# Expert matmuls in pairs of units: the fp32r products of both units first, then the bf16 products of both

## The chip, the cores and the metric

The kernel runs on one core of one Trainium2 chip. The metric is the device time of one execution in microseconds; before the change the median of three runs is 2556.29 us (2554.6 to 2564.03). A core has several engines, each with its own instruction queue that runs in order: TensorE (PE in the profile, with its weight loads as PEld) multiplies matrices into PSUM, ScalarE (ACT) and VectorE (DVE) work on tiles, GpSimd (POOL) issues the gathers and scatters here, SyncE (SP) issues the loads of weights. They synchronise by semaphores: an instruction raises a counter when it is done, and another queue waits for a value of it.

## The reference

One encoder layer for two request groups of 16 + 512 tokens with shared weights (float32, width 1024): a combined projection, differential attention, a bidirectional mLSTM, an output projection, and then the part that this change touches, a mixture of experts in which each expert chooses its tokens:

```python
aff = softmax(xt @ w_router)              # 16 experts
gate, idx = lax.top_k(aff.T, cap)         # cap = 66 tokens of each group
def expert(args):
    ids, wg, wu, wd = args                # (1024, 2816), (1024, 2816), (2816, 1024)
    xg = xt[ids]
    return (jax.nn.silu(xg @ wg) * (xg @ wu)) @ wd
y = zeros.at[idx].add(expert outputs * gate)
```

Each expert thus multiplies 132 rows (66 of each group) by two matrices of 1024 x 2816 and one of 2816 x 1024.

## The kernel before, in words

The change lies in `experts` (from L1591), the last stage. The kernel keeps float32 accuracy by splitting both operands. A weight w is split into a high half in the format fp32r (`whi`) and a rest in bf16 (`wlo`); the rows are split into a high and a low half in fp32r that stand side by side in `xx` (264 columns), with a bf16 copy of the rows in `xb` (132 columns). One product of weights is then two matmuls into the same PSUM bank: `whi` times the 264 columns in fp32r, and `wlo` times the 132 columns in bf16, added onto the first 132.

An expert is cut into 34 units (`UNITS`). Units 0 to 21 are "up" units: unit u = 2t + kind computes 256 columns of the gate matrix (kind 0) or of the up matrix (kind 1), as 2 x 8 matmuls of each format into two PSUM banks. An expert's up units use four of the eight banks (`bank_set`), so that unit u + 2 goes into the banks of unit u. Units 22 to 33 are "down" units, with 16 or 12 matmuls of each format; six of them add into one set of four banks (`dg` 0), six into the other (`dg` 1). What an up unit leaves is summed in two steps: ScalarE copies the right half of the two banks to `low` (`copy_low`, L1832), and VectorE adds the left half to it into `gs` or `us` (`add_low`, L1945), which raises `sum_ready`. Then ScalarE's silu (L1839) and VectorE's product (`gate`, L1951) make the hidden rows, which both engines split (L1844, L1845, L1957) for the down units.

The weights come in pieces of up to 2 MB through a ring of five `raw` buffers, issued by SyncE as soon as VectorE has done the last split of the piece that the buffer held. For each unit n ScalarE makes `whi` (`split_high`, L1822), and VectorE `wlo` from it (`split_low`, L1916). Both halves have rings of five (`R_SPLIT`), so split_high(n) waits until unit n - 5 is done.

The order of each queue is written out by hand. TensorE runs its units in order; an up unit waits for `sum_ready` of unit u - 2 (L1742), then for `whi`, and before its bf16 matmuls for `wlo` (L1752). After units 2 to 5 it transposes a part of the previous expert's outputs (`turn_outputs`, L1795), after unit 23 the next expert's rows (`turn_rows`, L1732). ScalarE and VectorE have a loop over the same steps u. In step u ScalarE does: copy_low(u - 1); split_high of the units up to `made(ex, u)` (L1650), which is u plus a lead of 4, 3 or 2 units (`lead`, L1646: 4 for u < 6 and u >= 30, 3 for 6 to 12 and 27 to 29, 2 for 13 to 26), so one unit in most steps, none in steps 6 and 13, two in steps 27 and 30; then silu in odd steps or the split of the hidden rows in even ones; then, in steps 3 to 6, `gated_rows` (L1877). VectorE does in step u: add_low(u - 1); `gate` in even steps; the split of the hidden rows in odd ones; and then split_low of the same unit as ScalarE's split_high of that step.

The code below has the line numbers of the profile.

Of the kernel before, what the change touches and what calls it, by code (L numbers as in the profile page):

```python
# [57 lines left out]
N_EXP = 16  # L58
# [87 lines left out]
def build(nc, x_meta, x_prompt, x_sample, g_mix, w_in, b_gates, conv_w, g_q, g_k, lams, g_da, g_ml,  # L146
          w_out, g_ffn, w_router, w_gate, w_up, w_down, rope_cos, rope_sin, out, xn_rows, zv_rows, stages=5):
    with ExitStack() as ctx:
# [70 lines left out]
        if stages >= 5:  # L219
            experts(nc, locals())  # L220
# [1044 lines left out]
UNITS_UP = 22  # L1265
DOWN_PARTS = ((0, 4), (4, 4), (8, 4), (12, 4), (16, 3), (19, 3))
UNITS = UNITS_UP + 2 * len(DOWN_PARTS)
# [323 lines left out]
def experts(nc, e):  # L1591
# [17 lines left out]
    low = [tiles(f"low{i}", [P, 2, C2]) for i in range(2)]  # L1609
# [30 lines left out]
    TURN_X = UNITS_UP + 1  # L1640
    SPLIT_X = TURN_X + 2
    DG0_END, DG1_END = UNITS_UP + 6, UNITS
    OUT_STEPS = {2: 0, 3: 1, 4: 2, 5: 3}
    FETCH, ADD = 13, 7

    def lead(u):  # L1646
# [7 lines left out]
    def bank_set(ex):  # L1654

        return 4 * (ex % 2)

    def other_set(ex):

        return 4 - bank_set(ex)  # L1660

    def shaped(t, u):

        cols = 256 if u < UNITS_UP else 512
        n = KD if u < UNITS_UP else DOWN_PARTS[(u - UNITS_UP) % 6][1]
        return t[:, 0:n * cols].rearrange("p (k f) -> p k f", f=cols)
# [5 lines left out]
    with nc.Block() as block:  # L1672

        @block.sync
        def _(sp):
            for q in range(NR, PIECES * N_EXP):
                ex, p = divmod(q - NR, PIECES)
                sp.wait_ge(lo_ready, UNITS * ex + LAST_UNIT[p] + 1)
                load_piece(sp, e, raw, loaded, q)
            sp.wait_ge(added, 32 * N_EXP)  # L1680
# [31 lines left out]
        @block.tensor  # L1712
        def _(pe):
            for c in range(NC5):
                at = PT + CCOL[c]
                mm = pe.transpose(banks(0, G * N_EXP)[:, at:at + CROWS[c]], AFF[0:CROWS[c], c], ident[0:CROWS[c], 0:CROWS[c]])  # L1716
            mm.then_inc(aT_done, 1)
            pe.wait_ge(ranked, 1)
            for i, t in enumerate((vals, indexf)):
                mm = pe.transpose(banks(2, CAP)[:, 32 * i:32 * i + 32], t[:, 0:CAP], ident[0:G * N_EXP, 0:G * N_EXP])  # L1720
            mm.then_inc(lists_done, 1)

            def turn_rows(ex):

                pe.wait_ge(xg_loaded, 32 * ex + 32)
                if ex >= 1:
                    pe.wait_ge(sum_ready, UNITS_UP * ex)
                b = other_set(ex)
                for k in range(KD):
                    for g in range(G):  # L1730
                        at = 512 * (k // 3) + (k % 3) * C2 + CAP * g
                        mm = pe.transpose(banks(b)[:, at:at + CAP], xg[:, g, k * P:(k + 1) * P], ident[0:CAP, 0:CAP])  # L1732
                mm.then_inc(xT_done, 1)

            def up(ex, u):

                t, kind = divmod(u, 2)
                n = UNITS * ex + u
                if t == 0 and kind == 0:
                    pe.wait_ge(xl_ready, ex + 1)  # L1740
                if t >= 1:
                    pe.wait_ge(sum_ready, UNITS_UP * ex + 2 * (t - 1) + kind + 1)  # L1742
                elif ex >= 1:
                    pe.wait_ge(yT_ready, 2 * ex - 1)
                pe.wait_ge(hi_ready, n + 1)
                b = bank_set(ex) + 2 * kind
                w = shaped(whi[n % R_SPLIT], u)
                for i in range(2):
                    for k in range(KD):
                        pe.matmul(banks(b + i)[:, 0:2 * C2], w[:, k, i * P:(i + 1) * P], xx[:, k], start=(k == 0), stop=False,  # L1750
                                  skip_group_check=True)
                pe.wait_ge(lo_ready, n + 1)  # L1752
                w = shaped(wlo[n % R_SPLIT], u)
                for i in range(2):
                    for k in range(KD):
                        mm = pe.matmul(banks(b + i)[:, 0:C2], w[:, k, i * P:(i + 1) * P], xb[:, k], start=False, stop=(k == KD - 1),  # L1756
                                       skip_group_check=True)
                mm.then_inc(unit_done, 1)

            def down(ex, u):  # L1760

                dg, d = divmod(u - UNITS_UP, len(DOWN_PARTS))
                c0, cn = DOWN_PARTS[d]
                n = UNITS * ex + u
                b = (other_set(ex), bank_set(ex))[dg]
                if d == 0 and dg == 0 and ex >= 1:
                    pe.wait_ge(yr_ready, 4 * ex)
                if d == 0 and dg == 1:
                    pe.wait_ge(sum_ready, UNITS_UP * (ex + 1))
                    if ex + 1 < N_EXP:  # L1770
                        pe.wait_ge(xl_ready, ex + 2)
                if dg == 0:
                    pe.wait_ge(hl_ready, PAIRS * ex + (c0 + cn + 1) // 2)
                pe.wait_ge(hi_ready, n + 1)
                w = shaped(whi[n % R_SPLIT], u)
                for c in range(cn):
                    for i in range(HD2):
                        pe.matmul(banks(b + i)[:, 0:2 * C2], w[:, c, i * P:(i + 1) * P], hx[:, c0 + c], start=(c0 + c == 0), stop=False,  # L1778
                                  skip_group_check=True)
                pe.wait_ge(lo_ready, n + 1)  # L1780
                w = shaped(wlo[n % R_SPLIT], u)
                for c in range(cn):
                    for i in range(HD2):
                        mm = pe.matmul(banks(b + i)[:, 0:C2], w[:, c, i * P:(i + 1) * P], hb[:, c0 + c], start=False,  # L1784
                                       stop=(c0 + c == M - 1), skip_group_check=True)
                mm.then_inc(unit_done, 1)

            def turn_outputs(ex, i):

                g, half = divmod(i, 2)  # L1790
                if i == 0:
                    pe.wait_ge(yT_ready, 2 * ex + 2)
                b = bank_set(ex) + i
                for k in range(HD2):
                    mm = pe.transpose(banks(b, CAP)[:, k * P:(k + 1) * P], yT[:, HD2 * half + k, CAP * g:CAP * (g + 1)], ident[:])  # L1795
                mm.then_inc(y_done, 1)

            turn_rows(0)
            for ex in range(N_EXP):
                for u in range(UNITS):  # L1800
                    if u < UNITS_UP:
                        up(ex, u)
                    else:
                        down(ex, u)
                    if u in OUT_STEPS and ex >= 1:
                        turn_outputs(ex - 1, OUT_STEPS[u])
                    if u == TURN_X and ex + 1 < N_EXP:
                        turn_rows(ex + 1)
            for i in range(4):
                turn_outputs(N_EXP - 1, i)  # L1810

        @block.scalar
        def _(act):
# [33 lines left out]
            def split_rows(ex):  # L1847

                act.wait_ge(xT_done, ex + 1)
                if ex >= 1:  # L1850
                    act.wait_ge(unit_done, UNITS * (ex - 1) + UNITS_UP)
                b = other_set(ex)
                two = banks(b)[:, 0:1024].rearrange("p (b n) -> p b n", b=2)[:, :, 0:3 * C2].rearrange("p b (k n) -> p b k n", k=3)
                one = banks(b + 2)[:, 0:2 * C2].rearrange("p (k n) -> p k n", k=2)
                for t in (xx, xb):
                    nc.scalar.activation(t[:, 0:6, 0:C2].rearrange("p (b k) n -> p b k n", b=2), two, ACT.Copy)
                    last = nc.scalar.activation(t[:, 6:8, 0:C2], one, ACT.Copy)
                last.then_inc(xh_ready, 1)
# [9 lines left out]
            def gated_rows(ex, i):  # L1868

                g, half = divmod(i, 2)  # L1870
                act.wait_ge(y_done, 4 * ex + i + 1)
                if i == 0:
                    if ex + 1 < N_EXP:
                        act.wait_ge(xT_done, ex + 2)
                    else:
                        act.wait_ge(added, 32 * ex)
                nc.scalar.activation(yr[:, g, 512 * half:512 * (half + 1)], banks(bank_set(ex) + i, CAP)[:, 0:512], ACT.Copy,  # L1877
                                     scale=gateT[:, g, ex:ex + 1]).then_inc(yr_ready, 1)
# [6 lines left out]
            for ex in range(N_EXP):  # L1885
                for u in range(UNITS):
# [13 lines left out]
                    if u == SPLIT_X and ex + 1 < N_EXP:  # L1900
                        split_rows(ex + 1)
                    if u - 1 in OUT_STEPS and ex >= 1:
                        gated_rows(ex - 1, OUT_STEPS[u - 1])
            copy_ylow(N_EXP - 1, 1)
# [126 lines left out]
```

## Time and profile before

| | us |
|---|---|
| median of three runs | 2556.29 |
| the profiled execution | 2560.51 |
| its span, first to last instruction | 2558.7 |
| TensorE matmuls, busy | 2412.1 (94%) |
| VectorE, busy | 1934.0 (76%) |
| ScalarE, busy | 1697.3 (66%) |
| split_low (`wlo`, L1916), 436 + 108 instructions | 963.6 + 240.5 |
| split_high (`whi`, L1822), 436 + 108 instructions | 804.9 + 201.5 |

Times in the profile are microseconds from the span's start. A row of the timeline gives the start, the length, the engine, the line of the code, the operation, what it writes and reads with shapes, how many instructions are merged (x16), and in brackets how long the engine was idle before it and what released it. A row of the busy times gives the stretch, its length, then for PE, PEld, DVE, ACT and POOL the busy time with the number of instructions, then the clock that TensorE was granted (1.00 is 2.4 GHz, 0.50 is 1.2 GHz), the busy share of the DMA engines and GB/s. A row of the waits gives who waited for whom: the total, how often, and the longest. The ends of matmuls are modelled, so starts, above all those of weight loads, are the better marks.

### The profile page before, as it was taken

Reading aid. Unit: us, or ns where it says so; the run is one execution under the profiler, and the core shown is the slowest. Engines: PE = TensorE matmul, PEld = TensorE weight load, DVE = VectorE, ACT = ScalarE, POOL = GpSimd, SP = SyncE. Lnnn points to the kernel's source line nnn. Section 1 sums busy time; section 2 is a strip of 40 time slices with the busy share of each in tenths; the row PEclk is TensorE's granted clock in tenths of the full one; section 3 lists DMA queues with packets and bytes.
Section 4 is the critical chain, followed back from the end, with each engine's and each line's share of the span. In section 5 each row is a group of like instructions: output and inputs, shape, how many; then the busy total and the mean of one; then the engine's idle time right before and its main releaser. Section 6 shows DMA issues by size and latency. Waiting matters only on the chain.

```text
span 2558.7 us, 51699 instructions
## 1 busy us (share of the span) xinstructions
PE 2412.1 (94%) x21830; PEld 2206.4 (86%) x21830; DVE 1934.0 (76%) x2311; ACT 1697.3 (66%) x2379; POOL 265.6 (10%) x174
## 2 busy tenths in 40 slices
PE   7999997998979929999999999999999999999997
PEld 5777884785757729999999999999999999999997
DVE  4621035884873359999998998998999999989986
ACT  7311224573443228888888888887888888888885
POOL 3312111110122010000000000000000000000000
PEclk9999996896889959999999999999999999999999
DMA  4122101001023359999999999999999999999993
GB/s 124 33 86 81 66 17 35 1 13 56 1 91 123 116 187 321 366 362 349 366 360 350 381 346 352 379 344 366 366 349 365 362 348 368 360 348 383 345 365 127
DMA packets 325114, 624.33 MB, mean 244 GB/s; under 512 B 11828, under 2 KB 48788, under 8 KB 324884
## 3 DMA queue, kind: packets, MB, share of 16 engines
q1 hardware_dynamic: 317220, 602.78, 66.2%
q0 software_dynamic: 7664, 18.25, 3.6%
q8 instruction: 173, 2.83, 0.5%
q14 instruction: 57, 0.47, 0.1%
HBM read 597.23 MB, written 23.69 MB: 243 GB/s over the span
## 4 chain that ended last, share of the span: by engine, by line
PE 59%; issue 3%; DVE 1%; DMA 1%; POOL 0%; ACT 0%; POOLq 0%
PE ps L1750 26%; PE ps L1778 13%; PE ps L1756 13%; PE ps L1784 6%; PE ps L1795 1%; PE ps L1732 1%; POOL xg L1693 0%; DMA xg<-xn_rows,idxT 0%; DVE vals L1924 0%; DVE index L1927 0%; DMA out_rows<-yr,idxT 0%; DVE aff L1926 0%; POOL out_rows L1701 0%; POOLq L1672 0%; PE ps L1716 0%
## 5 line engine op out<-in xcount | busy, mean ns | idle before, releaser
L1916 DVE TENSOR_TENSOR wlo<-raw,whi 128x2048 bf16<-128x2048 f32 (+1 forms) x436 | 963.6, 2223 | 55.0 <-ACT whi L1822 55.0
L1822 ACT ACTIVATE whi<-raw 128x2048 fp32r<-128x2048 f32 (+1 forms) x436 | 804.9, 1859 | 37.6 <-PE ps L1784 37.6
L1750 PE MATMUL ps<-xx,whi 128*128 128x264 f32 x4512 | 616.2, 289 | 3.6 <-DVE xx L1967 3.6
L1750 PEld LDWEIGHTS ps<-xx,whi 128*128 128x128 f32 x4512 | 564.2, 189 | 3.8 <-DVE xx L1967 3.8
L1756 PE MATMUL ps<-xb,wlo 128*128 128x132 bf16 x4512 | 313.7, 221 | 0.0
L1778 PE MATMUL ps<-hx,whi 128*128 128x264 f32 x2256 | 312.3, 290 | 0.0
L1778 PEld LDWEIGHTS ps<-hx,whi 128*128 128x128 f32 x2256 | 283.8, 189 | 0.0
L1756 PEld LDWEIGHTS ps<-xb,wlo 128*128 128x128 bf16 x4512 | 264.0, 97 | 13.8
L1916 DVE TENSOR_TENSOR wlo_last<-raw,whi_last 128x2048 bf16<-128x2048 f32 (+1 forms) x108 | 240.5, 2227 | 13.6 <-ACT whi_last L1822 13.6
L1832 ACT ACTIVATE low<-ps 128x264 f32<-128x264 f32 x352 | 137.7, 391 | 135.7 <-PE ps L1756 122.0
L1822 ACT ACTIVATE whi_last<-raw 128x2048 fp32r<-128x2048 f32 (+1 forms) x108 | 201.5, 1866 | 9.3 <-PE ps L1784 9.3
L1701 POOL DMA_INDIRECT out_rows<-yr,idxT x32 | 48.4, 1512 | 1235.8 <-ACT yr L1877 1231.0
L1784 PE MATMUL ps<-hb,wlo 128*128 128x132 bf16 x2256 | 157.0, 221 | 0.0
L1750 PE MATMUL ps<-xx,whi_last 128*128 128x264 f32 x1120 | 154.1, 290 | 0.0
L444 PE MATMUL ps<-w_hi,h_hi 128*128 128x512 f32 (+1 forms) x360 | 144.3, 401 | 4.5 <-POOL w_lo L314 4.5
L444 PE MATMUL ps<-w_hi,h_lo 128*128 128x512 f32 (+1 forms) x360 | 141.6, 393 | 0.0
L444 PE MATMUL ps<-w_lo,h_hi 128*128 128x512 f32 (+1 forms) x360 | 141.6, 393 | 0.0
L1750 PEld LDWEIGHTS ps<-xx,whi_last 128*128 128x128 f32 x1120 | 141.2, 189 | 0.0
L1784 PEld LDWEIGHTS ps<-hb,wlo 128*128 128x128 bf16 x2256 | 130.1, 98 | 7.7
L1945 DVE TENSOR_TENSOR gs<-ps,low 128x264 f32<-128x264 f32 x176 | 74.9, 426 | 30.7 <-ACT low L1832 30.7
L522 ACT ACTIVATE w_hi<-w 128x1024 fp32r<-128x1024 f32 x28 | 29.4, 1054 | 103.5 <-DMA w<-in_w_in 103.5
L671 DVE TENSOR_SCALAR cy<-zp,cols 128x1056 f32<-128x1056 f32 x8 | 6.2, 770 | 120.8 <-ACT zp L581 120.8
(236 smaller groups left out, 3463.4 us busy)
## 6 DMA issues: line engine op xcount, KB each, us to landing
raw<-in_w_gate SPq DMA_DIRECT2D x80, 2048.0 KB, 12.7
raw<-in_w_up SPq DMA_DIRECT2D x80, 2048.0 KB, 10.3
raw<-in_w_down SPq DMA_DIRECT2D x64, 2048.0 KB, 10.7
raw<-in_w_down SPq DMA_DIRECT2D x32, 1536.0 KB, 8.1
raw<-in_w_gate SPq DMA_DIRECT2D x16, 1024.0 KB, 9.0
raw<-in_w_up SPq DMA_DIRECT2D x16, 1024.0 KB, 11.6
w<-in_w_in SPq DMA_DIRECT2D x28, 512.0 KB, 4.9
zv_rows<-qn SPq DMA_DIRECT2D x24, 256.0 KB, 2.0
```

The source lines that it names most:

```text
L444: mm = pe.matmul(banks(4 + i % 3, ZROWS[c])[:, 0:512], h, w, start=(k == 0 and i3 == 0), stop=(k == KD - 1 and i3 == 2))
L522: nc.scalar.activation(w_hi[u % NW][:], w_whole[u % NW][:], ACT.Copy).then_inc(w_high, 1)
L1701: nc.gpsimd.indirect_dma_start(out, bass.IndirectOffsetOnAxis(ap=idxT[:, g, ex:ex + 1], axis=0), yr[:, g, :], None, compute_op=ALU.add).th ...
L1732: mm = pe.transpose(banks(b)[:, at:at + CAP], xg[:, g, k * P:(k + 1) * P], ident[0:CAP, 0:CAP])
L1750: pe.matmul(banks(b + i)[:, 0:2 * C2], w[:, k, i * P:(i + 1) * P], xx[:, k], start=(k == 0), stop=False, skip_group_check=True)
L1756: mm = pe.matmul(banks(b + i)[:, 0:C2], w[:, k, i * P:(i + 1) * P], xb[:, k], start=False, stop=(k == KD - 1), skip_group_check=True)
L1778: pe.matmul(banks(b + i)[:, 0:2 * C2], w[:, c, i * P:(i + 1) * P], hx[:, c0 + c], start=(c0 + c == 0), stop=False, skip_group_check=True)
L1784: mm = pe.matmul(banks(b + i)[:, 0:C2], w[:, c, i * P:(i + 1) * P], hb[:, c0 + c], start=False, stop=(c0 + c == M - 1), skip_group_check=True)
L1822: nc.scalar.activation(shaped(whi[n % R_SPLIT], u), unit_raw(raw, ex, u), ACT.Copy).then_inc(hi_ready, 1)
L1832: nc.scalar.activation(low[u % 2][:], src, ACT.Copy).then_inc(low_ready, 1)
L1916: nc.vector.tensor_tensor(shaped(wlo[n % R_SPLIT], u), unit_raw(raw, ex, u), shaped(whi[n % R_SPLIT], u).bitcast(F32), ALU.subtract).then_ ...
L1945: nc.vector.tensor_tensor((gs, us)[kind][:], src, low[kind][:], ALU.add).then_inc(sum_ready, 1)
```

## The change

On TensorE's queue `up` is cut into `up_high` (the fp32r matmuls, with the waits for the banks and for `whi`) and `up_low` (the wait for `wlo` and the bf16 matmuls, which raise `unit_done`); `down` likewise. The loop goes over pairs of units. The steps after which the outputs are transposed become the odd units 3, 5, 7 and 9; `OUT_STEPS` is also read by ScalarE, whose `gated_rows` move from steps 3 to 6 to steps 4, 6, 8 and 10. `TURN_X` is 23, so the next expert's rows are transposed at the same place as before. Nothing else of ScalarE's and VectorE's order changes, and each matmul is the same as before.

```diff
-    OUT_STEPS = {2: 0, 3: 1, 4: 2, 5: 3}
+    OUT_STEPS = {3: 0, 5: 1, 7: 2, 9: 3}
...
-            def up(ex, u):
+            def up_high(ex, u):
...
+            def up_low(ex, u):
+
+                n = UNITS * ex + u
                 pe.wait_ge(lo_ready, n + 1)
+                b = bank_set(ex) + 2 * (u % 2)
                 w = shaped(wlo[n % R_SPLIT], u)
...
-            def down(ex, u):
+            def down_high(ex, u):
...
+            def down_low(ex, u):
+
+                dg, d = divmod(u - UNITS_UP, len(DOWN_PARTS))
+                c0, cn = DOWN_PARTS[d]
+                n = UNITS * ex + u
+                b = (other_set(ex), bank_set(ex))[dg]
                 pe.wait_ge(lo_ready, n + 1)
                 w = shaped(wlo[n % R_SPLIT], u)
...
-                for u in range(UNITS):
-                    if u < UNITS_UP:
-                        up(ex, u)
-                    else:
-                        down(ex, u)
-                    if u in OUT_STEPS and ex >= 1:
-                        turn_outputs(ex - 1, OUT_STEPS[u])
-                    if u == TURN_X and ex + 1 < N_EXP:
+                for u in range(0, UNITS, 2):
+                    high, low = (up_high, up_low) if u < UNITS_UP else (down_high, down_low)
+                    high(ex, u)
+                    high(ex, u + 1)
+                    low(ex, u)
+                    low(ex, u + 1)
+                    if u + 1 in OUT_STEPS and ex >= 1:
+                        turn_outputs(ex - 1, OUT_STEPS[u + 1])
+                    if u + 1 == TURN_X and ex + 1 < N_EXP:
                         turn_rows(ex + 1)
```

## Rows read from the trace of the kernel before

**Rows 1.** Busy time of each engine, the expert stage.
```profile
948.00:2542.00 1594.00, 1594.00 (x17369) 1567.25 (x17370) 1465.54 (x1305) 1339.15 (x1571) 85.09 (x60) 1.00 1.00 350
```

**Rows 2.** Waits, 948 to 2545 us.
```profile
ACT low L1832 <- PE ps L1756: 122.0, 227, 5.3
...
DVE wlo L1916 <- ACT whi L1822: 55.0, 101, 1.4
```

**Rows 3.** Timeline of one pair of up units.
```profile
1770.25 0.94 PEld L1756 LDWEIGHTS ps<-xb,wlo_last 128*128 128x128 bf16 x16
...
1771.15 2.00 PEld L1750 LDWEIGHTS ps<-xx,whi 128*128 128x128 f32 x16
...
1771.40 0.39 ACT L1832 ACTIVATE low<-ps 128x264 f32<-128x264 f32 x1 [0.46 <-PE ps L1756]
1771.69 1.91 ACT L1822 ACTIVATE whi<-raw 128x2048 fp32r<-128x2048 f32 x1
...
1773.20 0.93 PEld L1756 LDWEIGHTS ps<-xb,wlo 128*128 128x128 bf16 x16
...
1773.49 0.41 ACT L1844 ACTIVATE hb<-hid 128x264 bf16<-128x264 f32 x1
1773.69 2.28 DVE L1916 TENSOR_TENSOR wlo<-raw,whi 128x2048 bf16<-128x2048 f32 x1
1773.80 0.41 ACT L1845 ACTIVATE hx<-hid 128x264 fp32r<-128x264 f32 x1
...
1775.89 0.43 DVE L1945 TENSOR_TENSOR gs<-ps,low 128x264 f32<-128x264 f32 x1
...
1776.13 0.93 PEld L1756 LDWEIGHTS ps<-xb,wlo 128*128 128x128 bf16 x16
```

**Rows 4.** The page's costliest groups: busy us, mean ns of one; weight loads.
```profile
L1750 PEld LDWEIGHTS ps<-xx,whi 128*128 128x128 f32 x4512 | 564.2, 189 | 3.8 <-DVE xx L1967 3.8
...
L1756 PEld LDWEIGHTS ps<-xb,wlo 128*128 128x128 bf16 x4512 | 264.0, 97 | 13.8
```

**Rows 5.** Timeline of a step in which VectorE waited for ScalarE twice.
```profile
1768.44 0.39 ACT L1832 ACTIVATE low<-ps 128x264 f32<-128x264 f32 x1 [1.74 <-PE ps L1756]
1768.73 1.91 ACT L1822 ACTIVATE whi<-raw 128x2048 fp32r<-128x2048 f32 x1
...
1768.86 0.43 DVE L1945 TENSOR_TENSOR gs<-ps,low 128x264 f32<-128x264 f32 x1 [1.75 <-ACT low L1832]
...
1770.67 2.29 DVE L1916 TENSOR_TENSOR wlo<-raw,whi 128x2048 bf16<-128x2048 f32 x1 [1.03 <-ACT whi L1822]
```

**Rows 6.** Timeline, the weight loads of one group of output transposes.
```profile
1754.86 0.39 PEld L1795 LDWEIGHTS ps<-ident,yT 128*66 128x66 f32 x4
```

**Rows 7.** Timeline, the first unit of the expert stage, at the low clock.
```profile
947.24 0.42 DVE L1967 TENSOR_TENSOR xx<-ps,xx 128x264 fp32r<-128x264 f32 x1
947.72 3.58 PEld L1750 LDWEIGHTS ps<-xx,whi 128*128 128x128 f32 x16 [3.76 <-DVE xx L1967]
...
951.40 1.71 PEld L1756 LDWEIGHTS ps<-xb,wlo 128*128 128x128 bf16 x16
...
953.08 2.07 PEld L1750 LDWEIGHTS ps<-xx,whi 128*128 128x128 f32 x16
```

**Rows 8.** Idle spans of TensorE in earlier stages, and busy time with clock by stretch.
```profile
469.71 0.50 PE L777 MATMUL ps<-k_hi,q_hi 64*128 64x264 f32 x2 [1.50 <-ACT prob L837]
...
488.51 0.51 PE L777 MATMUL ps<-k_hi,q_hi 64*128 64x264 f32 x2 [1.50 <-ACT prob L837]
...
889.74 1.10 PE L1445 MATMUL ps<-ident,xn 128*128 128x128 f32 x8 [2.62 <-DVE xn L1538]
...
472.00:478.00 6.00, 6.00 (x29) 5.24 (x29) 5.76 (x13) 3.00 (x9) 0.00 (x0) 0.50 0.01 3
489.10:499.00 9.90, 9.90 (x48) 8.82 (x47) 6.33 (x13) 4.91 (x15) 0.00 (x0) 0.50 0.01 2
887.00:897.00 10.00, 5.50 (x44) 4.23 (x44) 4.88 (x16) 2.82 (x11) 0.00 (x0) 1.00 0.73 255
```

## The prediction

> **What bounds the kernel now.** I read the busy time by stretch first. From 948 to 2542 us, the expert stage, TensorE is busy in every microsecond, at the full clock; VectorE is busy 92% of the stretch and ScalarE 84% [rows 1]. So this stage, 1594 of the 2558.7 us, is bound by TensorE, with VectorE close behind. The waits come next: ScalarE waits 122 us for bf16 products (its copy of the PSUM half) and VectorE 55 us for the fp32r halves that ScalarE makes [rows 2]. Both queues have some slack, and TensorE waits for neither. Then the timeline of one pair of up units shows how the three queues lock together [rows 3]. From the bf16 part of one unit (1770.25) to that of the unit after next (1776.13) is 5.88 us. A unit's 16 fp32r products take 2.05 us (1771.15 to 1773.20), its 16 bf16 products about 0.90.
>
> **What the change removes.** Two switches between the kinds per pair of units. An fp32r weight load lasts 189 ns [rows 4], so the 16 of 2.00 us follow each other every (2.00 - 0.19)/15 = 0.121 us; 16 such steps are 1.93, and the first bf16 load comes 0.12 later than that. For bf16, (0.93 - 0.10)/15 = 0.0555, 16 steps 0.89, and nearly nothing is lost [rows 3, 4]. The trace shows no fp32r unit after another, so the gain is bounded: 0 if the 0.12 us belongs to the wait instruction, which stays, and 0.13 per pair if it is the switch. I take 0.12; with 8 x 34 = 272 pairs (16 experts of 34 units) it is at most 272 x 0.12 = 33 us.
>
> **What it adds.** A PSUM bank pair is free again for unit u+2 when sum_ready of unit u is there (the copy on ScalarE and then the addition on VectorE). Until now the next unit's 2.94 us lay between the end of unit u and its bank's next use. Now, in front of pair (u+2, u+3), only the 0.89 us of up_low(u+1) lies there. Nothing else can run meanwhile: behind the waiting up_high on TensorE's queue stand the rest of the pair, the output transposes and all later units, and ScalarE's next copies wait for those.
>
> I work out one steady cycle of the up stage, u even, zero at the first weight load of up_low(u):
> - TensorE: up_low(u) to 0.89, up_low(u+1) to 1.78.
> - ScalarE starts copy_low(u) at 1.15 (1770.25 to 1771.40) and split_high 0.29 later, at 1.44, for 1.91: until 3.35 [rows 3]. copy_low(u+1) stands behind that split and silu in the program's order, at 3.24 + 0.31 = 3.55. The 1.80 and 0.31 used here are start to start of a split and of a small operation (1771.69 to 1773.49, 1773.49 to 1773.80) [rows 3].
> - VectorE starts add_low(u) 0.42 after copy_low's start, at 1.57, and takes 0.43: sum_ready(u) at 2.00 [rows 5]. TensorE starts 0.06 after the addition that releases it (947.24 + 0.42 to 947.72) [rows 7]: up_high(u+2) at 2.06 instead of 1.78, a stall of 0.28, and it ends at 3.99.
> - VectorE's next large work is the split_low of the same step, which stands ahead of add_low(u+1). It needs the fp32r half from ScalarE: 0.03 after 3.35 (1768.73 + 1.91 to 1770.67) [rows 5], so 3.38, and add_low(u+1) starts 2.20 later (1773.69 to 1775.89) [rows 3], at 5.58, until 6.01.
> - up_high(u+3) therefore starts at 6.07, a stall of 2.08, takes 2.04, and the next cycle begins at 8.11.
>
> The rest fits in: ScalarE's second split (3.84 to 5.75) and its hidden-row split end near 6.4, VectorE's gate and second split near 8.7, before the next copy at 9.26 and addition at 9.68. So the cycle is 8.11 against 5.88, 2.23 more. What has changed is that split_low waits behind copy_low(u), which waits for TensorE; before, VectorE's queue was full enough that its splits ran beside the matmuls.
>
> An expert has ten such boundaries between up pairs. Behind unit 12 the look-ahead drops from 3 to 2, step 13 makes no split, and add_low(13) is ready at 3.2: only the 0.28 is left and the cycle is 6.03. So 16 x 9 = 144 cycles cost 2.23, +321 us, and 16 cost 0.15, +2. The output transposes, 4 x 15 = 60 groups of 0.39 [rows 6], move to behind a pair and fall into the stall: -23. The six down pairs and the last up pair of each expert keep their gain of 0.12, 112 x 0.12 = -13; in the down stage nothing waits for sums pair by pair, and its splits arrive before they are read (the closest, split_low(23), ends at 3.38 + 2.29 = 5.67 in the cycle of units 20 and 21, and down_low(23) starts at 1.78 + 1.93 + 2.04 + 0.89 = 6.64), so I cost the moved waits there at nothing; if VectorE ran late, each would cost up to a split, 2.28. Loads are issued behind split_low, later than now, but each has a longer cycle to land. Sum: 321 + 2 - 23 - 13 = +287.
>
> **The clock.** TensorE now stands still for 2.08 us in each of those cycles. The trace has three idle spans of that order in stretches that otherwise run at the full clock: 1.50 us before 469.71, 1.50 before 488.51 and 2.62 before 889.74 [rows 8]. After the first two the granted clock was 0.50 (1.2 GHz) from 472 to 478 and from 489.1 to 499; after the third it stayed at 1.00 [rows 8]. Two of three: I let the clock fall in 96 of the 144 cycles. What a fall costs is read from the first unit of the stage, at the low level: 3.68 us for the fp32r part, 1.68 for the bf16 part (947.72, 951.40, 953.08), 1.8 and 1.9 times the 2.04 and 0.89 of full clock [rows 7]. The low stretches begin 0.6 and 2.3 us after work resumed [rows 8]; of the 2.93 us from up_high(u+3) to the end of up_low(u+2), 0.6 to 2.3 are then left and run at the low level. That adds 0.5 to 2.0; I take 1.3. Beyond that point slowness only eats the next stall. 96 x 1.3 = +125.
> The Trainium skill, TensorE: Matmul & The Clock Gate, section "A second HAM failure mode: psum-queue depth-cycling", says that a kernel which cycles through PSUM banks can idle in short gaps often enough that the clock swings between its two levels. By that rule the clock falls here, as in the sum; the two falls agree with it, the third span does not.
>
> **The sum.** The profiled run took 2560.5 us, 4.2 more than the median of 2556.3 (span 2558.7 in it). 2560.5 + 287 + 125 = 2972; against the median, 2968.
>
> **Rivals.**
> - The same stalls with a steady clock: 2556 + 287 = 2843. For it: the idle span of 2.62 us that left the clock alone, and dense full-array work on both sides of each stall. Against it: the two falls after 1.50.
> - The clock stays low through the up stage. The cycle with 3.68 and 1.68: up_low pair to 3.36, copy at 2.01, split to 4.21, VectorE's split to 6.52, sum_ready(u+1) at 6.86, up_high(u+3) from 6.92 to 10.6. No stall is left, but 10.6 - 5.88 = 4.72 per cycle: 144 x 2.49 more than the 287, 3202 us. Against it: TensorE would then be busy throughout, and after 478 and 499 such work brought the clock back.
> - Faster: the splits run so far ahead that VectorE never stands behind ScalarE's current one. It decides whether sum_ready(u+1) comes before 3.99, 2.0 us earlier than I find. Then each boundary costs 0.15 at most: 160 x 0.15 - 23 - 13 = -12, 2544; with the 0.28 gone too, 2556 - 33 = 2523. For it: VectorE waits only 55 us for fp32r halves in the whole stage [rows 2], and a ring of five halves leaves room. Against it: both queues put copy_low(u) and add_low(u) ahead of the split of their step, so nothing of that step can start before TensorE has finished up_low(u).
>
> **How the numbers follow.** Stalls with falls of the clock 0.60 (own range 2900 to 3050), with a steady clock 0.28 (2830 to 2880, with a little for each restart), clock low throughout 0.05, faster or no change 0.07. The range 2830 to 3050 holds the first two but for a small part and leaves out the others. Half a per cent is what a measurement of this kernel can tell from no change: faster by more 0.04 (the 2523 end), within 0.03 (2544 and misses above it), slower 0.93.
>
> **What would show it.** Right: TensorE's idle time before L1750 of about 2.1 us in 144 places, put down to the VectorE addition of the odd unit (us), near 300 us in all, and 0.28 us in 160 places put down to gs; VectorE's wait of split_low for whi grown from 55 us by about 1 us per cycle (2.34 to 3.38); the down stage of an expert shorter by under 1 us; output transposes no longer on the path; stretches of granted clock between 0.5 and 1 in the up stage. Wrong: no idle time of TensorE in the stage (the third rival); a clock of 1.00 throughout (the first); cycles with the long stall in step 13 too, or stalls in the down stage, which would mean that I have the order of the queues wrong.

## The result, and the profile after

The changed kernel takes 2902.44 us (median of six runs, 2900.95 to 2909.5) against 2558.47 for the kernel before in the same comparison: a ratio of 1.1348, 95% interval 1.1329 to 1.1368. It is 344 us slower. The forecast was 2968, its range 2830 to 3050.

The busy times of the expert stage, columns as in [rows 1]:

```profile
948.00:2888.00 1940.00, 1688.70 (x17368) 1626.34 (x17369) 1484.84 (x1307) 1315.78 (x1571) 97.89 (x60) 0.97 0.84 288
```

The stage is 1940 us long instead of 1594, and TensorE is idle in 251 of them; before it was idle in none [rows 1]. VectorE and ScalarE are busy for about as long as before (1485 and 1316 us against 1466 and 1339 [rows 1]), so they too now stand still for longer. The granted clock is 0.97 on average, no longer 1.00. The waits of the stage say for whom:

```profile
ACT low L1845 <- PE ps L1761: 534.4, 176, 7.1
PEld ps L1750 <- DVE us L1958: 264.1, 144, 2.1
DVE gs L1958 <- ACT low L1845: 249.2, 161, 5.2
DVE wlo L1929 <- ACT whi L1835: 146.8, 152, 1.4
...
PEld ps L1750 <- DVE gs L1958: 33.2, 93, 1.2
```

TensorE waits in exactly 144 places for the addition of the odd unit (`us`). ScalarE's wait for the bf16 products has grown from 122 to 534 us, VectorE's wait for fp32r halves from 55 to 147 [rows 2]: each queue waits for the next in a ring. The timeline of one cycle shows the ring, from the bf16 part of a pair at 963.24:

```profile
963.24 1.87 PEld L1761 LDWEIGHTS ps<-xb,wlo 128*128 128x128 bf16 x32
964.39 0.39 ACT L1845 ACTIVATE low<-ps 128x264 f32<-128x264 f32 x1 [3.52 <-PE ps L1761]
964.68 1.90 ACT L1835 ACTIVATE whi<-raw 128x2048 fp32r<-128x2048 f32 x1
964.81 0.43 DVE L1958 TENSOR_TENSOR gs<-ps,low 128x264 f32<-128x264 f32 x1 [0.99 <-ACT low L1845]
965.30 1.99 PEld L1750 LDWEIGHTS ps<-xx,whi_last 128*128 128x128 f32 x16 [0.19 <-DVE gs L1958]
...
966.61 2.29 DVE L1929 TENSOR_TENSOR wlo<-raw,whi 128x2048 bf16<-128x2048 f32 x1 [1.37 <-ACT whi L1835]
966.79 0.38 ACT L1845 ACTIVATE low<-ps 128x264 f32<-128x264 f32 x1
...
968.82 0.42 DVE L1958 TENSOR_TENSOR us<-ps,low 128x264 f32<-128x264 f32 x1
...
969.30 1.99 PEld L1750 LDWEIGHTS ps<-xx,whi 128*128 128x128 f32 x16 [2.01 <-DVE us L1958]
```

Read it downwards: the copy of the even unit starts 1.15 us after the bf16 part, ScalarE's split right behind it, VectorE's split the moment that one ends (966.61, after 1.37 us of waiting), the addition of the odd unit behind that (968.82), and TensorE after 2.01 us of standing still (969.30). The next pair's bf16 part starts at 971.34, 8.10 after this one; before it was 5.88 [rows 3].

Some cycles are longer. One of them, by the weight loads of its timeline:

```profile
973.40 2.00 PEld L1750 LDWEIGHTS ps<-xx,whi 128*128 128x128 f32 x16 [0.19 <-DVE gs L1958]
977.40 3.17 PEld L1750 LDWEIGHTS ps<-xx,whi 128*128 128x128 f32 x16 [2.01 <-DVE us L1958]
980.69 2.17 PEld L1761 LDWEIGHTS ps<-xb,wlo 128*128 128x128 bf16 x32
```

And the busy times of three stretches of it, where the column behind POOL's is the granted clock:

```profile
977.00:978.00 1.00, 0.59 (x4) 0.60 (x5) 0.78 (x3) 0.00 (x0) 0.00 (x0) 0.96 0.05 18
979.00:980.00 1.00, 1.00 (x6) 1.00 (x6) 0.00 (x0) 0.00 (x0) 0.00 (x0) 0.50 0.00 0
982.00:984.00 2.00, 1.99 (x25) 1.81 (x23) 0.77 (x2) 1.86 (x2) 0.00 (x0) 1.00 0.00 0
```

The 16 weight loads behind the stall take 3.17 instead of 1.99 us: the clock is at its low level from about 978 to 981. The 144 long stalls have 143 distances between them, by the starts of the fp32r parts behind them. 34 of these are longer by about 1.55 us (9.4 to 9.7 instead of 8.1 where one long stall directly follows another); the others agree within 0.1. Behind the last stall, which no other follows, the loads are slow too, a 35th fall:

```profile
2850.98 2.90 PEld L1750 LDWEIGHTS ps<-xx,whi 128*128 128x128 f32 x16 [2.00 <-DVE us L1958]
```

The falls are not spread evenly. This is a cycle in which TensorE transposes a part of the previous expert's outputs (L1807):

```profile
1090.61 0.39 PEld L1807 LDWEIGHTS ps<-ident,yT 128*66 128x66 f32 x4
1091.00 2.00 PEld L1750 LDWEIGHTS ps<-xx,whi 128*128 128x128 f32 x16
...
1094.85 1.99 PEld L1750 LDWEIGHTS ps<-xx,whi_last 128*128 128x128 f32 x16 [1.85 <-DVE us L1958]
```

The transposes fill the even unit's stall, and 1.85 us of idle time are left. In none of the 60 cycles of this kind did the clock fall, nor in the first up cycle of experts 1 to 15, where the idle time comes in two parts (1.2 and 1.0 us). All 35 falls follow one of the other 69 stalls, of 2.0 us. Expert 0, which has no outputs to transpose, has falls behind units 7 and 9, where the other experts have none.

### The profile page after: what moved, and what is told of

It is laid out like the page before. It is cut to its first block, busy times and chain, and to the rows that moved or that the text cites. A ratio compares the mean times of both kernels' runs of the same rounds, so it can differ in the third digit from the quotient of the medians.

```text
span 2904.6 us, 51699 instructions
## 1 busy us (share of the span) xinstructions
PE 2506.9 (86%) x21830; PEld 2265.8 (78%) x21830; DVE 1952.8 (67%) x2311; ACT 1672.8 (58%) x2379; POOL 278.2 (10%) x174
## 4 chain that ended last, share of the span: by engine, by line
PE 40%; issue 12%; ACT 9%; DVE 6%; DMA 1%; POOL 0%; ACTq 0%; POOLq 0%
PE ps L1750 16%; PE ps L1783 11%; ACT whi L1835 7%; PE ps L1761 7%; PE ps L1796 5%; DVE wlo L1929 2%; DVE us L1958 2%; ACT whi_last L1835 2%; DVE wlo_last L1929 1%; PE ps L1732 1%; POOL xg L1693 0%; DMA xg<-xn_rows,idxT 0%; DMA out_rows<-yr,idxT 0%; DVE vals L1937 0%; DVE index L1940 0%
## 5 line engine op out<-in xcount | busy, mean ns | idle before, releaser
L1750 PE MATMUL ps<-xx,whi 128*128 128x264 f32 x4512 | 646.6, 299 | 203.6 <-DVE us L1958 186.8
L1750 PEld LDWEIGHTS ps<-xx,whi 128*128 128x128 f32 x4512 | 591.0, 197 | 241.1 <-DVE us L1958 211.0
L1783 PE MATMUL ps<-hx,whi 128*128 128x264 f32 x2256 | 296.3, 287 | 0.0
L1761 PEld LDWEIGHTS ps<-xb,wlo 128*128 128x128 bf16 x4512 | 285.5, 102 | 8.7
L1701 POOL DMA_INDIRECT out_rows<-yr,idxT x32 | 68.2, 2132 | 1679.7 <-ACT yr L1890 1674.8
L1796 PE MATMUL ps<-hb,wlo 128*128 128x132 bf16 x2256 | 146.7, 221 | 0.0
L837 ACT ACTIVATE prob<-ps,nmax 128x528 f32<-128x528 f32 (+1 forms) x80 | 55.2, 693 | 62.2 <-DVE nmax L934 62.1
## 6 DMA issues: line engine op xcount, KB each, us to landing
raw<-in_w_up SPq DMA_DIRECT2D x80, 2048.0 KB, 10.9
```

Source lines behind the costliest of these rows:

```text
L837: nc.scalar.activation(prob[i % 2][j][0:R, :], banks(2 * j, R)[:, PH:PH + T], ACT.Exp, bias=nmax[0:R, i % 2, j:j + 1], accum_out=lsum[0:R, ...
L1701: nc.gpsimd.indirect_dma_start(out, bass.IndirectOffsetOnAxis(ap=idxT[:, g, ex:ex + 1], axis=0), yr[:, g, :], None, compute_op=ALU.add).th ...
```

## The experiments

The theory under test: the loss is the order of the queues in the up stage (the addition of the odd unit stands behind a split that waits for ScalarE), plus the clock; the pairs themselves save a little. The rivals: the way from TensorE over ScalarE and VectorE and back is too long whatever the order; or pairing slows the products themselves.

**Pairs in the down units alone** (up units one by one, transposes at their old places):

```diff
+                for u in range(UNITS_UP):
+                    up_high(ex, u)
+                    up_low(ex, u)
...
+                for u in range(UNITS_UP, UNITS, 2):
+                    down_high(ex, u)
+                    down_high(ex, u + 1)
+                    down_low(ex, u)
+                    down_low(ex, u + 1)
```

> Pairs in the down units alone, the up units one by one as before, output transposes after units 2 to 5 as before. Theory (the up stage's queues make the loss; the switch between the two kinds of product costs 0.12 us and pairing saves it): 6 pairs x 16 experts x 0.12 = 11.5 us faster than before, about 2547 us against 2558, ratio 0.9955, TensorE never idle in the expert stage. Rival 1 (the 0.12 us belongs to the wait for the bf16 half, which stays): 2558, no change. Rival 2 (pairing itself makes the products slower, by weight loads or banks, wherever it is done): slower than before by several us or more.

Measured: 2566.68 us against 2556.73, ratio 1.0034 (1.0021 to 1.0046), 10 us slower. The theory missed here, and by the time alone the second rival would be right. The trace shows the pairs of down units at 5.79 us (first fp32r load to first fp32r load of the next) against 5.87 before, so they do gain, 0.08 and not 0.12. The loss is in another place, the third unit of the following expert, in 15 experts (timeline of the first such bank wait in one):

```profile
1857.58 0.70 DVE L1991 TENSOR_TENSOR yT<-ps,ylow 128x528 f32<-128x528 f32 x1
...
1858.20 2.28 DVE L1931 TENSOR_TENSOR wlo<-raw,whi 128x2048 bf16<-128x2048 f32 x1
...
1860.40 0.42 DVE L1960 TENSOR_TENSOR gs<-ps,low 128x264 f32<-128x264 f32 x1
...
1860.87 1.76 PEld L1750 LDWEIGHTS ps<-xx,whi 128*128 128x128 f32 x14 [1.17 <-DVE gs L1960]
```

Two down units end close together, so their halves of the ring come free late; VectorE reaches the new expert with a split still ahead of its first addition, and TensorE waits 1.17 us.

**The same with VectorE's lead at 2 units throughout**, so that this split comes later:

```diff
+    def made_dve(ex, u):
+        return min(UNITS * N_EXP, UNITS * ex + u + 3)
...
-                    while ahead < made(ex, u):
+                    while ahead < made_dve(ex, u):
```

> Pairs in the down units alone, and VectorE's lead set to 2 units in every step (ScalarE's leads as they were), so that at the start of an expert no splits of later units stand ahead of the first addition. Theory (the pairs do save 0.08 us each, 5.79 against 5.87, but pairs end together, VectorE's splits for the next expert come late, and the first up bank waits 1.15 us for its addition in 15 experts): that wait goes, 96 x 0.08 = 7.7 us less than before, about 2549, ratio 0.997. Rival (pairing of the down units costs elsewhere, the wait only shows it): the wait moves to another unit and the time stays at 2566.

Measured: 2549.16 against 2557.99, ratio 0.9964 (0.9951 to 0.9978). TensorE is again busy in all of the stage:

```profile
960.00:2530.00 1570.00, 1570.00 (x17208) 1548.34 (x17206) 1453.38 (x1297) 1322.53 (x1560) 136.76 (x60) 1.00 1.01 355
```

This version beats both kernels, if by a third of a per cent only. Whether the lead alone does it was tried with single units (the same edit of `made` in the kernel before):

> The kernel before with VectorE's lead set to 2 units in every step and nothing else; no pairs. Control for the version with pairs in the down units and the same lead. Theory (the lead only takes away a wait that pairs bring; without pairs TensorE waits for nothing): no change, 2556 to 2560. Rival (the lead itself is worth the 9 us): about 2549.

Measured: 2556.85 against 2556.32, ratio 1.0004 (0.9995 to 1.0013): the lead alone is worth nothing, the 9 us belong to the pairs with this lead. In the traces the down units of all experts together, by their weight loads, take 527.2 us with pairs and 533.8 without, so about 7 of the 9 are seen there.

**Only ScalarE's queue reordered** in the changed kernel:

```diff
+                    if 2 <= u <= UNITS_UP and u % 2 == 0:
+                        copy_low(ex, u - 2)
                         copy_low(ex, u - 1)
+                        silu(ex, u // 2 - 1)
...
```

(the splits of both steps follow; VectorE's next addition gets a wait that is always met).

> The changed kernel with only ScalarE's queue reordered: both copies, silu, then the two splits, with the leads as they were; VectorE's order as in the change. Theory: ScalarE's split of the step now starts behind the second copy (2.67 instead of 1.44 us after the start of the first bf16 part), VectorE's split follows it (4.61 to 6.9), the addition of the odd unit ends at 7.24 instead of 6.01 and the cycle is 9.34 instead of 8.10: 144 x 1.24 = 179 us slower than the change, 3081, although the copies come earlier; with a stall of 3.3 us the clock may fall oftener, up to 3180. Rival (ScalarE's late copy of the odd unit makes the stall): faster than the change, by up to 144 x 1.5 = 216 us, 2690.

Measured: 3310.61 against 2556.73, ratio 1.2941 (1.2921 to 1.2961): 408 us slower than the change, although ScalarE's copies come earlier. That settles which wait ends last:

```profile
1905.72 3.70 ACT L1839 ACTIVATE whi<-raw 128x2048 fp32r<-128x2048 f32 x2
1907.66 2.29 DVE L1933 TENSOR_TENSOR wlo<-raw,whi 128x2048 bf16<-128x2048 f32 x1 [2.28 <-ACT whi L1839]
...
1909.87 0.42 DVE L1964 TENSOR_TENSOR us<-ps,low 128x264 f32<-128x264 f32 x1
...
1910.35 3.38 PEld L1754 LDWEIGHTS ps<-xx,whi 128*128 128x128 f32 x16 [3.24 <-DVE us L1964]
```

VectorE's split waits 2.28 us for ScalarE's, and TensorE stalls 3.24. The time lies above the expected range: most cycles are 10.7 to 10.9 us and not 9.34, since with this stall the clock falls in nearly every cycle (the loads above take 3.38 us). One cycle of each expert, the first behind the boundary without a long stall, is 9.36, as worked out. 144 x 1.24 for the queue and some 110 more falls of 1.5 make 344; of the other 64 us, about 11 are waits of down units for `whi` and about 20 come from cycles of 12.1 to 12.2, one in each expert; the rest I have not traced.

**Only VectorE's queue reordered**, both additions ahead of the two splits:

```diff
+                    if 2 <= u <= UNITS_UP and u % 2 == 0:
+                        add_low(ex, u - 2)
+                        if u >= 6:
+                            split_hid(ex, (u - 6) // 2)
                         add_low(ex, u - 1)
+                        gate(ex, u // 2 - 1)
...
```

> The changed kernel with only VectorE's queue reordered: both additions of a pair ahead of the two splits; ScalarE's order as in the change. Theory: the addition of the odd unit waits for ScalarE's second copy (3.94) and no longer for the split (5.67); then VectorE's own work (5.9 us a pair plus its wait) sets the cycle, by turns 6.5 and 7.1 us, 6.8 on average: 144 x 1.3 = 187 us less than the change and, with stalls under 1.5 us, the 53 us of the clock too: 2665, or 2720 if the clock still falls. Rival (only the order of ScalarE's queue counts): 2900.

Measured: 2682.56 against 2557.99, ratio 1.049 (1.0469 to 1.0512). 220 us of the 344 are gone by moving additions past splits on one engine; about 54 of them are the clock's, which no longer falls (it is 1.00 from 960 to 2660 us). The waits of the stage show what is left:

```profile
DVE us L1958 <- ACT low L1845: 169.1, 176, 2.0
PEld ps L1750 <- DVE gs L1958: 120.2, 145, 1.3
```

VectorE now waits about 1 us per pair for ScalarE's late second copy and falls behind; the cycles are by turns 6.5 and 7.1 us, as worked out, and TensorE waits for the even unit instead.

**Both queues reordered, ScalarE up to two units further ahead** (the two edits above together, and a lead of 4 for ScalarE's splits):

```diff
+    def made_act(ex, u):
+
+        return min(UNITS * N_EXP, UNITS * ex + u + 5) if u <= 20 else made(ex, u)
```

> The changed kernel with another order in ScalarE's and VectorE's queues: in an even step of the up stage both copies (both additions) come first, then the splits of the two steps, and ScalarE makes its halves two units further ahead (lead 4 up to unit 20), so that VectorE's split finds its half ready. Nothing is left out. Theory (the 2.0 us stall is the addition of the odd unit standing behind a split that waits for ScalarE): the stall put down to the us addition goes, the cycle of a pair is 6.0 to 6.1 us instead of 8.10, 144 x 2.05 = 295 us less and the clock's long cycles with it (53 us): 2554, within 15 of before. Rival (the stall is the way from TensorE over ScalarE and VectorE back, whatever the order of the queues): about 2900, as the changed kernel.

Measured: 2610.89 against 2556.73, ratio 1.0209 (1.0195 to 1.0223). That is 57 us above the theory's 2554. The wait for `us` is gone and most cycles are 6.03 to 6.23; but three cycles at the start of each expert are about 7.1, as VectorE's lead is 4 there too and its splits again follow ScalarE's of the same step. With VectorE's lead at 2 throughout:

> Pairs everywhere, both queues reordered, ScalarE with a lead of 4 up to unit 20 and VectorE with a lead of 2 throughout, so that VectorE's splits never follow ScalarE's of the same step. Theory (the cycles of 7.13 us at the start of each expert, three of ten, are those in which both leads were 4): all ten cycles 6.0 to 6.15 us, 160 x 0.2 = 32 us more than before, transposes hidden in part (16 less), 112 pairs with 0.08 less (9): about 2565, TensorE waiting some 0.2 us per pair for the addition of the even unit and nowhere for that of the odd one. Rival (those cycles are long for another reason, the output rows or loads at the start of an expert): 2611 as before this edit.

Measured: 2566.47 against 2557.99, ratio 1.0034 (1.0022 to 1.0046). All cycles are 6.0 to 6.4 us, but for the first of the stage, and one wait of TensorE in the up stage is left:

```profile
PEld ps L1758 <- DVE gs L1968: 24.8, 101, 0.4
```

Nearly the whole loss of the change has gone, with all units in pairs and only the order and lead of two other queues edited. It is still not faster than single units: by the starts of the loads the up units of all experts take 1077.8 us (1061.4 before) and the down units 527.1 (533.8 before). In the up units VectorE, the third column of busy times, now has hardly any slack:

```profile
1858.00:1912.00 54.00, 53.68 (x574) 52.33 (x572) 51.91 (x52) 47.71 (x62) 6.93 (x4) 1.00 0.99 333
```

It is busy 96% of this stretch of up units. That this is why pairs gain nothing there is likely, but no run shows it.

**The stall filled.** 28 matmuls of 132 bf16 columns between the fp32r parts:

```diff
+                    if 2 <= u < UNITS_UP and u != 14:
+                        fill(ex, u)
```

> The changed kernel with 28 more bf16 matmuls of 132 columns (28 x 0.0555 = 1.55 us) between the fp32r parts of the two units of a pair, where TensorE stands still for 2.0 us; they write columns of the bank that nobody reads; not in pair 0 and pair 7 of an expert, which have no long stall. Theory (34 cycles are 1.55 us longer than 8.10 because the clock falls after the stall): no cycle above 8.2 us but the one with the first unit of the kernel, the granted clock 1.00 in the stage, 34 x 1.55 = 53 us less than the change, about 2850. Rival (the long cycles have another cause, a transfer or a split): they stay, 2900. If the added matmuls don't fit into the stall, each 0.1 us beyond it costs 14 us.

(The added matmuls write into a bank that holds an open sum, and with them the output is not the layer's; how they disturb it was not isolated. The run is read for its times alone.) Measured: 2857.94 against 2556.73, ratio 1.1172 (1.1154 to 1.1189), 44.5 us less than the change with 4032 matmuls more. The busy times of the stage with the clock, and one filled stall in the timeline:

```profile
960.00:2850.00 1890.00, 1855.24 (x21271) 1794.63 (x21268) 1476.30 (x1300) 1312.68 (x1569) 100.57 (x62) 1.00 0.86 296
```

```profile
1908.19 2.01 PEld L1750 LDWEIGHTS ps<-xx,whi 128*128 128x128 f32 x16
1910.24 1.63 PEld L1759 LDWEIGHTS ps<-xb,wlo 128*128 128x128 bf16 x28
1912.04 2.00 PEld L1750 LDWEIGHTS ps<-xx,whi 128*128 128x128 f32 x16 [0.16 <-DVE us L1969]
```

The clock is 1.00 throughout and the cycles are 8.1 us. So the long cycles of the change are the clock's, and nothing else's. One reason why the gain is 44.5 and not 53 us is that the added work was put into the first up cycle of every expert too, where the odd unit's stall is 1.0 us in 15 of them and not 2.0: the distance over the down units, from the last long stall of an expert to the first of the next, is 47.6 us against 46.9 in the change without a fall, 15 x 0.7 = 10.5 us.

## Why the prediction was right, and where it was off

- **The steady cycle.** Worked out 8.11 us; 94 of the 143 distances are 8.09 to 8.13, and the other ordinary ones are within 0.1 of it or have a fall of the clock on top. 144 x 2.22 = 320 us. Each link stands in the timeline above at its worked-out distance: copy 1.15, addition 1.57, fp32r 2.06, split 3.37, odd addition 5.58, odd fp32r 6.06. The experiments show that the order of the queues makes it: moving only the additions takes most of it away, moving only the copies makes it worse. TensorE's waits for `us` sum to 264 us in the 144 forecast places, near the 300 forecast. The small stall of the even unit is 0.19 and not 0.28, and stands in fewer places than 160, as the output transposes fill it.
- **Step 13** has no long stall, as forecast: the boundary behind it is 6.03 us (1010.48 to 1016.51), 16 times, +2.
- **The output transposes** no longer show: cycles with and without them are 8.10 us long. -23, right by that.
- **The switches** were mis-sized. Pairs of down units save 0.08 us and not 0.12, so 112 pairs give back 9 us, not 13. Where the other 0.04 goes was not separated.
- **The down stage.** "I cost the moved waits there at nothing" holds in the change only because the up stage's stall is longer: the wait of 1.2 us at the start of an expert lies inside the first cycle, which is 8.10 as well (1080.69 to 1088.79). Without that cover it cost 17 us in the kernel with pairs in the down units alone. My own steps would have shown VectorE late there; I looked at whether the splits are in time for TensorE and not at what stands behind them on VectorE.
- **The clock** is the term that was wrong by most: 96 falls of 1.3 us, +125; measured 35 of 1.55, +54. The price of a fall was near; the count, from three idle spans in other stages, was not. Three cases were too few for a share, and idle spans alone were not the thing to count. The trace of before also has falls with no idle span that the profile shows, as from 640 to 645 us, where TensorE is busy throughout at a mean clock of 0.76:

```profile
640.00:645.00 5.00, 5.00 (x23) 4.31 (x22) 3.22 (x13) 2.53 (x7) 0.00 (x0) 0.76 0.00 0
```

The prediction also treated the output transposes and the clock as separate terms. In the trace they hang together: the 60 cycles with transposes in the stall had no fall, and the other 84 had all 35. No run separates the transposes from the place of these cycles in the expert, but expert 0, without them, fell in the same places.

The sum with the measured terms: 320 + 2 - 23 - 9 + 54 = 344, against 346 between the two profiled spans (2558.7 and 2904.6). Without the clock it is 290, where the forecast had 287.

Of the rivals, the one with a steady clock (2843) was nearer in its clock than the forecast, though falls there were; the clock never stayed low (that rival's cycle should have been 10.72 and not 10.6 us, as its up_high(u+2) ends only at 3.36 + 3.68 = 7.04); and the faster one fell by exactly the order of the two queues that spoke against it. The rule of the Trainium skill that I set beside the clock (TensorE: Matmul & The Clock Gate, "A second HAM failure mode: psum-queue depth-cycling") agrees with this trace in kind: the clock swings, in 35 of 144 cycles.

## What to carry to other kernels

Before reordering one engine's queue, walk one cycle through all the queues that hand work to each other, with what stands behind each waiting instruction: here a gain of 0.08 us per pair on TensorE cost 2.2 us, because VectorE's and ScalarE's hand-written orders fitted the old sequence. Here almost all of the loss went when both engines that empty the banks put both drains of a pair ahead of their long background work, and VectorE's splits no longer followed ScalarE's of the same step; on ScalarE alone the same order made it worse. Look for the gain in the stage where the engine that is helped is the only bound: in the down units pairs gained 0.08 us each, in the up units even the best order gained nothing.

## What the runs showed of the hardware that was not expected

The clock's answer to a repeated stall is steep. With stalls up to 1.3 us in a cycle (VectorE's queue reordered) the granted clock stayed at 1.00 through the stage; with 2.0 us (the change) it fell to 0.50 in 35 of 144 cycles, and with 1.85 us (the cycles with output transposes) in none of 60; with 3.2 us (ScalarE's queue reordered) in nearly all. Each fall cost about 1.55 us here, and the low level lasted 3 to 4 us. Filling the 2.0 us with matmuls whose result nobody needs made the changed kernel 44.5 us faster.
